# One layer of a hybrid decoder (sparse attention, gated delta rule, S5, MLP) on one core: another layout of the S5 input, another order of the parameter work, the state stores and the attention bursts

## The chip, the cores and the metric

The program runs on one core of one Trainium2 chip. The metric is the device time of one execution in microseconds; the median of three runs of the kernel before is 2086.05 (2082.03 to 2086.13). Engines are named as in the profile: PE (TensorE) multiplies matrices, PEld is its weight load, DVE is VectorE, ACT is ScalarE, POOL is GpSimd, SP is SyncE, which issues most DMAs.

## The reference

A prompt of 1024 tokens and eight samples of eight tokens (1088 tokens in all, width 1024) go through one layer with the same weights:

- `h = rmsnorm(x)`; one projection `h @ w_in` gives the columns of three mixers.
- Attention, 8 query heads on 2 key/value heads of 64: a compressed branch over means of blocks of 64 keys, a selected branch over the best 16 blocks, a window of 512; three softmaxes with ALiBi, added by gates. With 1024 prompt tokens there are 16 blocks, so the selected branch sees every block before the query.
- A gated delta rule (4 heads of 64) behind a short convolution over four tokens; the last three pre-convolution rows of each sequence are outputs (the convolution states).
- S5, 16 groups of 16 channels with 64 complex states each: `h_t = A h_{t-1} + B u_t`, `y_t = Re(C h_t) + D u_t`, then GELU and a gated linear unit. The last states are outputs.
- `x += concat(mixers) @ w_out`, `x += relu(rmsnorm(x) @ up)^2 @ down`, a last rmsnorm. Key/value rows, window buffers and states are outputs too.

Everything is float32; large products are split into three products of rounded parts (high x high, low x high, high x low).

## The kernel before

The program is a row of blocks, each with one instruction stream for each engine and a barrier behind it: input norm with the feature projection and S5 (`feature_and_s5`, to 251 us of the profile), query projection with the short convolution (from 280), token projection, delta rule, sample attention, prompt attention (`prompt_attention`, some 915 to 1184), then the output projection and the MLP (`project_and_mlp`). Nothing plans the order: each engine runs its stream in the order in which it is written, and semaphores hold it.

**Projections** (`project`, lines 437 to 510). A weight chunk of 128 columns is loaded by SP into one raw buffer, rounded by ScalarE into the high part (line 458) and subtracted by VectorE into the low part (line 475); the next chunk is loaded after that. A unit is one chunk times one of three column groups of the tokens (`GROUPS_N`), 24 matmuls (lines 393 to 395). With the first unit of a chunk ScalarE and VectorE make the next chunk. Units 0 to 5 are the two chunks of S5's input u, units 6 to 23 the six chunks of the delta rule's q, k and v. ScalarE evicts each unit from one of three PSUM banks (line 642).

**S5** is woven between the units by `S5.scalar`, `S5.vector`, `S5.tensor` and `S5.pool`. It works on blocks of eight tokens: 128 blocks of the prompt and 8 of the samples. VectorE makes the angles, the powers of A, and the input matrix from 13 loaded parameters (`angles`, `powers`, `input_matrix`), ahead of all units (`vector_first`, `scalar_first`). GpSimd makes C times the powers of A (lines 759 to 769) when the powers are there. VectorE makes B times the powers at unit 3 (`input_powers`, line 916), the phases of the blocks at unit 6, the scan over blocks at unit 9. TensorE multiplies after unit 10 (prompt) and 12 (samples) the input with B (`products`, line 1063), in four tiles of 32 rows, and after unit 16 the outputs (`outputs`): the input with a table of taps (line 1073, 128 x 128 weights) and the states with C times the powers (line 1078, four column tiles of 32). The input `uT` is laid down token by token; both lines read token t of every block, a step of eight elements.

**Stores** at the end of this block (`stores`): SP waits for the last eviction, issues one DMA for the prompt's and six for the samples' convolution states out of the work array, then the two S5 states, and waits until all have landed.

**Prompt attention** goes by units (tile of 128 queries, one of four head pairs), 32 in all. A round e, written out by `schedule`, has for each score piece (up to 512 keys) of unit e: TensorE's scores of the two key/value heads (line 1822), VectorE's bias and row maximum (line 1907), ScalarE's exponentials; and for unit e - 2: groups of two key steps, each turned by four transposes (line 1847), copied to SBUF by ScalarE or, every third, VectorE, and multiplied with the values one group later (line 1833). The last group of a unit is multiplied at once and the compressed branch is added (line 1856). Two PSUM banks take the transposes, two the output, four the scores. Between scores and transposes VectorE makes the factors of unit e - 1 in round e behind the rows of the first piece (line 1918), and then scales one of the four stretches of probabilities, GpSimd three (line 1991).

## Time and profile before

| what | us |
| --- | --- |
| median of the runs | 2086.05 |
| the profiled execution | 2087.14 |
| its span, first to last instruction | 2085.3 |
| PE busy | 1838.9 (88%) |
| PEld busy | 1618.2 (78%) |
| DVE busy | 927.3 (44%) |
| ACT busy | 545.1 (26%) |
| POOL busy | 394.7 (19%) |

The times of rows are those of the profiled execution, counted from the first instruction of its span; what lies around the span is 1.84 us. The share of an engine is a mean over the whole span. A matmul's duration in a row holds its passage through the array; how fast they follow one another is read from their starts. A float32 matmul is two instructions.

### The profile page before, as it was taken

What the parts mean: (1) busy time and instruction counts of PE and PEld (TensorE: products, weight loads), DVE (VectorE), ACT (ScalarE), POOL (GpSimd) and SP (SyncE); (2) the same over time, 40 slices, a digit from 0 to 9 for tenths busy, and PEclk for the clock granted to TensorE, in tenths of its full rate; (3) what the DMA queues carried; (4) which work ended last, traced back from release to release, by engine and by line L of the source; (5) the groups of instructions that cost most, each with busy time, mean ns of one, the idle gap of its engine ahead of it and who ended that gap; (6) DMA issues with size and microseconds to landing.
All of it is one profiled execution on the core that took longest, in us unless ns stands there. A gap on an engine that the chain in (4) does not pass through costs nothing. (4 is left out here: it accounts for less than half of the span.)

```text
span 2085.3 us, 29782 instructions
## 1 busy us (share of the span) xinstructions
PE 1838.9 (88%) x12570; PEld 1618.2 (78%) x12570; DVE 927.3 (44%) x1767; ACT 545.1 (26%) x1069; POOL 394.7 (19%) x337
## 2 busy tenths in 40 slices
PE   6599868945999976668999799999999999999998
PEld 5598768945888866455555599988888899999986
DVE  6850054102444442235666435345544444444447
ACT  5111122112222212226565503321111111111122
POOL 2300000003344320016666300200000011111110
PEclk8789979976999986559999999999999999999999
DMA  3000241032000002010000210111111111111112
GB/s 126 30 22 11 12 54 42 22 112 81 1 1 1 26 2 69 10 71 1 1 2 1 78 51 23 56 54 41 41 41 41 42 60 41 41 41 41 41 41 86
DMA packets 35327, 81.30 MB, mean 39 GB/s; under 512 B 13658, under 2 KB 21946, under 8 KB 29914
## 3 DMA queue, kind: packets, MB, share of 16 engines
q1 hardware_dynamic: 32690, 73.53, 11.8%
q10 hardware_dynamic: 1976, 4.92, 0.6%
q8 instruction: 99, 1.62, 0.3%
q0 software_dynamic: 528, 0.95, 0.2%
q14 instruction: 34, 0.28, 0.0%
HBM read 71.36 MB, written 10.12 MB: 39 GB/s over the span
## 5 line engine op out<-in xcount | busy, mean ns | idle before, releaser
L393 PE MATMUL ps<-mlp_mix_hi,mlp_w_hi 128*128 128x364 f32 (+1 forms) x768 | 252.2, 328 | 0.0
L394 PE MATMUL ps<-mixT_lo,mlp_w_hi 128*128 128x364 f32 (+1 forms) x768 | 252.0, 328 | 0.0
L395 PE MATMUL ps<-mlp_mix_hi,w_lo 128*128 128x364 f32 (+1 forms) x768 | 251.7, 328 | 0.0
L2428 DVE TENSOR_TENSOR x<-x,ps 128x512 f32<-128x512 f32 (+1 forms) x288 | 181.4, 656 | 140.8 <-PE ps L395 139.3
L2408 POOL TENSOR_TENSOR mlp_rect<-mlp_rect 128x364 f32<-128x364 f32 (+1 forms) x96 | 77.7, 809 | 779.6 <-ACT mlp_rect L2350 779.6
L395 PE MATMUL ps<-mlp_w_hi,mlp_hid_lo 128*128 128x512 f32 x512 | 203.1, 397 | 0.0
L394 PE MATMUL ps<-w_lo,mlp_hid_hi_lo 128*128 128x512 f32 x512 | 202.9, 396 | 0.0
L393 PE MATMUL ps<-mlp_w_hi,mlp_hid_hi_lo 128*128 128x512 f32 x512 | 202.9, 396 | 0.0
L1991 POOL TENSOR_SCALAR pa_probs<-pa_probs,pa_fac 128x640 f32<-128x640 f32 (+7 forms) x96 | 159.2, 1671 | 222.2 <-DVE pa_fac L1918 222.2
L2350 ACT ACTIVATE mlp_rect<-ps 128x364 f32<-128x364 f32 (+1 forms) x96 | 45.7, 476 | 557.2 <-PE ps L395 554.3
L2468 DVE TENSOR_TENSOR mlp_hid_lo<-mlp_rect,mlp_hid_hi_lo 128x364 fp32r<-128x364 f32 x64 | 53.2, 831 | 234.4 <-ACT mlp_hid_hi_lo L2356 234.4
L393 PEld LDWEIGHTS ps<-mlp_mix_hi,mlp_w_hi 128*128 128x128 f32 x768 | 144.9, 189 | 0.7
L394 PEld LDWEIGHTS ps<-mixT_lo,mlp_w_hi 128*128 128x128 f32 x768 | 144.4, 188 | 0.6
L395 PEld LDWEIGHTS ps<-mlp_mix_hi,w_lo 128*128 128x128 f32 x768 | 144.2, 188 | 0.0
L393 PEld LDWEIGHTS ps<-mlp_w_hi,mlp_hid_hi_lo 128*128 128x128 f32 x512 | 96.5, 188 | 23.6
L394 PEld LDWEIGHTS ps<-w_lo,mlp_hid_hi_lo 128*128 128x128 f32 x512 | 96.5, 188 | 23.6
L395 PEld LDWEIGHTS ps<-mlp_w_hi,mlp_hid_lo 128*128 128x128 f32 x512 | 96.4, 188 | 23.5
L1833 PE MATMUL ps<-pa_PT,tokens 128*64 128x128 f32 x1056 | 89.2, 290 | 16.9 <-DVE pa_PT L1930 13.0
L2003 ACT ACTIVATE pa_probs<-pa_probs,pa_nm 128x640 f32<-128x640 f32 (+7 forms) x128 | 92.8, 728 | 31.6 <-DVE pa_nm L1907 31.6
L1847 PEld LDWEIGHTS ps<-ident,pa_probs 128*128 128x128 f32 x528 | 57.1, 144 | 56.5 <-issue 52.3
L1258 POOL TENSOR_TENSOR dn_B<-dn_AT,dn_level 128x512 f32<-128x512 f32 (+1 forms) x59 | 73.6, 1264 | 127.9 <-DVE dn_aqkT L1393 47.9
L2418 DVE TENSOR_TENSOR w_lo<-w_raw,mlp_w_hi 128x2048 fp32r<-128x2048 f32 x36 | 82.4, 2288 | 24.9 <-ACT mlp_w_hi L2325 24.9
(465 smaller groups left out, 3862.5 us busy)
## 6 DMA issues: line engine op xcount, KB each, us to landing
w_raw<-in_w_up SPq DMA_DIRECT2D x16, 1024.0 KB, 4.7
w_raw<-in_w_down SPq DMA_DIRECT2D x16, 1024.0 KB, 4.7
feat_raw<-in_w_feat SPq DMA_DIRECT2D x12, 512.0 KB, 3.6
uT<-in_w_token SPq DMA_DIRECT2D x4, 1056.0 KB, 5.3
ck<-in_cache_nsa SPq DMA_DIRECT2D x16, 256.0 KB, 3.0
w_raw<-in_w_out SPq DMA_DIRECT2D x4, 1024.0 KB, 6.5
x<-in_x_prompt SPq DMA_DIRECT2D x4, 1024.0 KB, 8.3
out_y_p<-x SPq DMA_DIRECT2D x8, 512.0 KB, 2.6
```

The lines of the kernel that those rows point to most:

```text
L393: pe.matmul(out, lhs[0], rhs[0], start=first, stop=False)
L394: pe.matmul(out, lhs[0], rhs[1], start=False, stop=False)
L395: return pe.matmul(out, lhs[1], rhs[0], start=False, stop=last)
L1258: pool.tensor_tensor(B[:n, x, :, :n], AT[:n, k % 4, :, :n], mask, ALU.mult).then_inc(b_ready, 1)
L1833: last = pe.matmul(m.ps[64 * g:64 * g + 64, 6 + i % 2, r * P:(r + 1) * P], values[:, g * HD:(g + 1) * HD], PT[:, st % PTN, (2 * s + g) * P ...
L1847: last = pe.transpose(m.ps[:, 4 + st % 2, (2 * s + g) * P:(2 * s + g + 1) * P], probs[:, slot(e, g), col:col + P], m.ident[:])
L1991: last = pool.tensor_scalar(probs[:, x, o:o + w], probs[:, x, o:o + w], fac[:, x, b:b + 1], None, ALU.mult)
L2003: act.activation(probs[:, x, o:o + w], probs[:, x, o:o + w], ACT.Exp, bias=nm[:, x, b, pieces(i)[j][1]:pieces(i)[j][1] + 1], scale=-1.0, a ...
L2408: pool.tensor_tensor(part, part, part, ALU.mult).then_inc(rect_squared, 1)
L2418: dve.tensor_tensor(w_lo[:, s, :], w_raw[:, s, :], w_hi[:, s, :], ALU.subtract).then_inc(w_lo_made, 1)
L2428: dve.tensor_tensor(part, part, bank, ALU.add).then_inc(done, 1)
L2468: dve.tensor_tensor(hid_lo[:, g % 2, f, o:o + w], part, hi, ALU.subtract).then_inc(hidden_lo, 1)
```

## The change

- `GROUPS_N` becomes 368, 360 and 360 columns wide, multiples of eight.
- S5's input is laid down with the token's place in its block as the outer index: the six evictions of units 0 to 5 read PSUM with a step of eight, and the products and outputs read contiguous blocks.
- The S5 parameters move from ahead of unit 0 to behind the eviction of unit 0 on ScalarE, and behind the rounding of the second weight chunk on VectorE.
- GpSimd's C powers move to VectorE (`output_powers`, at unit 6, behind the fourth chunk); the phases move from unit 6 to unit 7.
- The S5 states are stored before the last load of SP in the block. GpSimd copies the convolution states into two small arrays, feature chunk by feature chunk behind the evictions, and two DMAs store them. The block waits for the S5 states alone; SP of the query block waits for the other two at its end.
- In prompt attention a round has batches: up to two score pieces, up to three groups of transposes, then the values of the batch before. Three PSUM banks take the transposes and one the output; six slots instead of four hold the turned probabilities. The factors follow the rows of the first batch. ScalarE evicts a tile's output in the first batch of the next unit.

```diff
-GROUPS_N = [(0, 364), (364, 364), (728, 360)]
+GROUPS_N = [(0, 368), (368, 360), (728, 360)]
...
             sp.dma_start(m.token_raw[0], m.w_in[FEAT]).then_inc(m.token_raw[1], 16)
+            sp.wait_ge(m.sem("proj_stored"), 16 * 2)
...
             if c < 2:
-                dst = m.uT[:, c, o:o + w]
+                dst = s5.uT[:, c, :, o // 8:(o + w) // 8]
+                src = src.rearrange("p (b t) -> p t b", t=8)
...
+            s5.store(sp)
             sp.wait_ge(evac[0], len(units) - 2)
             sp.dma_start(m.query_raw[0][:], m.w_in[0]).then_inc(m.query_raw[1], 16)
-            sp.wait_ge(evac[0], len(units))
-            sp.wait_ge(conv_put, 7)
-            sp.dma_start(m.conv_prompt, m.dnx[:, :, SEQ:SEQ + 3]).then_inc(stored, 16)
-            for f in range(6):
-                sp.dma_start(m.conv_sample[:, f],
-                             m.dnx[:, f, 3 + SEQ:].rearrange("p (b s) -> p b s", b=NB)[:, :, NQ:NQ + 3]
-                             ).then_inc(stored, 16)
-            s5.store(sp)
-            sp.wait_ge(stored, 16 * 7)
+            sp.wait_ge(conv_kept, 12)
+            sp.dma_start(m.conv_prompt, m.conv_last[:]).then_inc(conv_stored, 16)
+            sp.dma_start(m.conv_sample, m.convbuf[:]).then_inc(conv_stored, 16)
+            sp.wait_ge(s5.stored, 32)
...
             s5.pool(pool)
+            pool.wait_ge(conv_put, 7)
+            for f in range(6):
+                pool.wait_ge(evac[0], 3 * (f + 2) + 3)
+                pool.tensor_copy(m.conv_last[:, f], m.dnx[:, f, SEQ:SEQ + 3]).then_inc(conv_kept, 1)
+                pool.tensor_copy(m.convbuf[:, f], m.dnx[:, f, 3 + SEQ:].rearrange("p (b s) -> p b s", b=NB)[:, :, NQ:NQ + 3]
+                                 ).then_inc(conv_kept, 1)
...
     def scalar(self, act, u):
         m = self.m
+        if u == 0:
+            self.scalar_params(act)
...
     def vector(self, dve, u):
+        if u == 0:
+            self.link = Link(dve, self.vec)
+            self.angles(dve)
+            self.powers(dve)
+            self.input_matrix(dve)
         if u == 3:
             self.input_powers(dve)
         if u == 6:
+            self.output_powers(dve)
+        if u == 7:
             self.phases(dve)
...
+    def output_powers(self, dve):
+
+        T, ca, cw, t, tt, link = self.T, self.ca, self.cw, self.hold_t, dve.tensor_tensor, self.link
+        c = lambda ri: self.over_k(cw[:, ri], T)
+        dve.wait_ge(self.neg_made, 1)
+        for ri, op in ((0, ALU.add), (1, ALU.subtract)):
+            tt(ca[:, ri], c(ri), self.power(0, 1, T + 1), ALU.mult)
+            link(tt(t, c(1 - ri), self.power(1, 1, T + 1), ALU.mult))
+            last = tt(ca[:, ri], ca[:, ri], t, op)
...
-                                         self.m.uT[rows, ct, tokens.start + t:tokens.stop:self.T], start=t == 0, stop=t == self.T - 1,
+                                         self.uT[rows, ct, t, blocks], start=t == 0, stop=t == self.T - 1,
...
-                pe.matmul(bank[:, e * n:(e + 1) * n], self.tb[:, ct, t, :], self.m.uT[:, ct, p - t::self.T],
+                pe.matmul(bank[:, e * n:(e + 1) * n], self.tb[:, ct, t, :], self.uT[:, ct, p - t, :],
...
-        PTN = 4
+        PTN, TURNS = 6, 3
...
-            if e >= len(UNITS):
-                return [(None, range(n))]
-            k = len(pieces(UNITS[e][0]))
-            return [(j, range(n * j // k, n * (j + 1) // k)) for j in range(k)]
+            k = len(pieces(UNITS[e][0])) if e < len(UNITS) else 0
+            parts = max((k + 1) // 2, (n + TURNS - 1) // TURNS)
+            return [(range(min(k, 2 * j), min(k, 2 * j + 2)), range(n * j // parts, n * (j + 1) // parts)) for j in range(parts)]
...
-                    if k == 0 and r == 0 and i >= 2:
-                        pe.wait_ge(o_out, i - 1)
+                    if k == 0 and r == 0 and i:
+                        pe.wait_ge(o_out, i)
...
+                held = []
                 for e in ROUNDS:
...
-                    for j, ks in schedule(e):
-                        if j is not None:
+                    for js, ks in schedule(e):
+                        for j in js:
                             scores(e, j)
                         for k in ks:
                             turn(e - LAG, k)
+                        for k in held:
+                            multiply(*k)
+                        held = [(e - LAG, k) for k in ks]
...
-                    for j, ks in schedule(e):
-                        if j is not None:
+                    for n, (js, ks) in enumerate(schedule(e)):
+                        for j in js:
                             rows(e, j)
-                        if (j or 0) == 0 and 1 <= e <= len(UNITS):
+                        if n == 0 and 1 <= e <= len(UNITS):
                             factors(e - 1)
                             scale(e - 1)
...
+                        if e - LAG - 1 >= 0 and UNITS[e - LAG - 1][1] == R - 1 and ks and ks[0] == 0:
+                            outputs(UNITS[e - LAG - 1][0])
```

## Rows read from the trace of the kernel before

**Rows 1.** Waits of PE, 0 to 300 us: total us, times, longest.
```profile
PE ps L393 <- DVE qp_wlo L475: 29.8, 1, 29.8
PE ps L393 <- DVE fp_wlo L475: 26.6, 1, 26.6
```

**Rows 2.** Timeline of DVE, S5 parameters: start, us, instruction.
```profile
49.18 3.51 DVE L890 TENSOR_TENSOR s_v<-s_par 128x8 f32<-128x8 f32 x1
...
56.32 0.17 DVE L892 TENSOR_TENSOR s_v<-s_v 128x8 f32<-128x8 f32 x1
```

**Rows 3.** Timeline of POOL at the same time, of ACT at unit 4.
```profile
49.03 3.64 POOL L764 TENSOR_TENSOR mixT_raw<-s_cw,s_ak 128x2048 f32<-128x2048 f32 x1 [19.51 <-DVE s_ak L876]
...
87.76 0.48 ACT L642 ACTIVATE uT<-ps 128x364 f32<-128x364 f32 x1 [3.52 <-PE ps L395]
```

**Rows 4.** Timelines at the block barriers near 278 and 331 us.
```profile
267.51 0.43 SPq L745 DMA_DIRECT2D out_s_s<-s_fin_s  x1
277.98 1.06 ACT L458 ACTIVATE qp_whi<-feat_raw 128x1024 fp32r<-128x1024 f32 x1 [26.89 <-PEq L437]
...
329.84 1.07 DVE L562 TENSOR_SCALAR qT<-ps 64x360 f32<-64x360 f32 x2 [2.23 <-PE ps L395]
331.20 0.33 POOL L538 MEMSET tokens<- 64x288 f32 x1 [52.18 <-POOLq L437]
```

**Rows 5.** Windows: length, PE, PEld, DVE, ACT, POOL busy (instructions), PEclk, DMA, GB/s.
```profile
77.30:82.00 4.70, 4.67 (x15) 4.67 (x16) 0.00 (x0) 1.05 (x1) 0.00 (x0) 0.50 0.33 112
83.10:107.80 24.70, 24.70 (x161) 24.65 (x160) 24.01 (x52) 7.73 (x17) 0.00 (x0) 1.00 0.14 44
143.50:151.50 8.00, 8.00 (x156) 8.00 (x152) 7.62 (x10) 0.00 (x0) 0.00 (x0) 0.50 0.01 4
940.00:1184.00 244.00, 229.08 (x1972) 137.90 (x1970) 141.02 (x480) 138.13 (x301) 148.30 (x81) 0.99 0.01 1
```

**Rows 6.** Groups of DVE, B times the powers: busy us, mean ns, idle before.
```profile
L916 DVE TENSOR_TENSOR s_bat<-s_bb,s_ak 128x1792 f32<-128x1792 f32 x2 | 4.0, 2021 | 0.0
```

**Rows 7.** Timeline of PE in the S5 outputs.
```profile
174.76 7.64 PE L1073 MATMUL ps<-uT,s_bat 128*128 128x136 f32 x30
182.33 1.60 PE L1078 MATMUL ps<-s_hp,mixT_raw 128*32 128x136 f32 x48
183.86 7.65 PE L1073 MATMUL ps<-uT,s_bat 128*128 128x136 f32 x30
```

**Rows 8.** Groups, 0 to 330 us: S5 products of the prompt.
```profile
L1063 PE MATMUL ps<-uT,s_bat 32*128 32x128 f32 x256 | 15.2, 408 | 0.0
```

**Rows 9.** Timeline of PE in attention, tile 5, and its last unit.
```profile
1088.16 0.66 PE L1847 MATMUL ps<-ident,pa_probs 128*128 128x128 f32 x4
1088.74 0.66 PE L1833 MATMUL ps<-pa_PT,tokens 128*64 128x128 f32 x8
1089.33 1.13 PE L1822 MATMUL ps<-kwinT,qT 64*128 64x512 f32 x4
1090.39 0.66 PE L1847 MATMUL ps<-ident,pa_probs 128*128 128x128 f32 x4
...
1175.60 1.09 PE L1847 MATMUL ps<-ident,pa_probs 128*128 128x128 f32 x8
```

**Rows 10.** Waits of PE, 905 to 1185 us.
```profile
PE ps L1833 <- DVE pa_PT L1930: 13.0, 25, 1.9
```

**Rows 11.** Groups of attention: score rows on DVE, scaling on POOL.
```profile
L1907 DVE CUSTOM_DVE_ANT_0 pa_probs<-ps,pa_dwin 128x512 f32<-128x512 f32 x40 | 26.0, 688 | 10.7 <-PE ps L1822 10.7
...
L1991 POOL TENSOR_SCALAR pa_probs<-pa_probs,pa_fac 128x640 f32<-128x640 f32 x36 | 68.8, 1921 | 13.6 <-DVE pa_fac L1918 13.6
```

**Rows 12.** Timeline of DVE: factors of units 8, 24 and 31.
```profile
953.61 0.16 DVE L1918 TENSOR_TENSOR pa_fac<-pa_rs,tokens 128x4 f32<-128x4 f32 x1
...
1087.40 0.16 DVE L1918 TENSOR_TENSOR pa_fac<-pa_rs,tokens 128x4 f32<-128x4 f32 x1
...
1165.42 0.16 DVE L1918 TENSOR_TENSOR pa_fac<-pa_rs,tokens 128x4 f32<-128x4 f32 x1
```

More of the change, by code:

```diff
@@ L607, in feature_and_s5 @@
     with ExitStack() as ctx:
[L608 to L609 removed]
+        conv_in, conv_put, conv_kept = m.sem("conv_in"), m.sem("conv_put"), m.sem("conv_kept")
+        conv_stored = m.sem("proj_stored")
         units = [(c, n) for c in range(8) for n in range(3)]
@@ L719, in __init__ @@
         sem = lambda n: m.sem(f"s5_{n}")
-        self.loaded, self.vec, self.vec_pool, self.e1, self.e2 = (sem(n) for n in ("loaded", "vec", "vec_pool", "e1", "e2"))
+        self.loaded, self.vec, self.e1, self.e2 = (sem(n) for n in ("loaded", "vec", "e1", "e2"))
         self.trig_in, self.trig, self.neg_made = sem("trig_in"), sem("trig"), sem("neg_made")
@@ L921, in input_powers @@
         last.then_inc(self.ba_made, 1)
+    def output_powers(self, dve):
[6 more added lines that the diff above has]
+            last = tt(ca[:, ri], ca[:, ri], t, op)
+            if ri == 0:
+                link(last)
+        last.then_inc(self.ca_made, 1)
     def phases(self, dve):
@@ L1019, in tensor @@
             pe.wait_ge(self.u_out[0], 6)
-            self.products(pe, slice(0, SEQ), self.NBLK).then_inc(self.g_prod, 1)
+            self.products(pe, slice(0, self.NBLK), self.NBLK).then_inc(self.g_prod, 1)
         if u == 11:
@@ L1033, in tensor @@
             pe.wait_ge(self.g_read, 1)
-            self.products(pe, slice(SEQ, TOK), NB).then_inc(self.gs_prod, 1)
+            self.products(pe, slice(self.NBLK, self.COLS), NB).then_inc(self.gs_prod, 1)
         if u == 16:
@@ L1053, in tensor, with products @@
                 last.then_inc(self.glu, 1)
-    def products(self, pe, tokens, n):
+    def products(self, pe, blocks, n):
         for ri in range(2):
@@ L1832, in multiply @@
                         for g in range(G):
-                            last = pe.matmul(m.ps[64 * g:64 * g + 64, 6 + i % 2, r * P:(r + 1) * P], values[:, g * HD:(g + 1) * HD],
+                            last = pe.matmul(m.ps[64 * g:64 * g + 64, 7, r * P:(r + 1) * P], values[:, g * HD:(g + 1) * HD],
                                              PT[:, st % PTN, (2 * s + g) * P:(2 * s + g + 1) * P], start=k + s == 0, stop=False,
@@ L1836, in multiply @@
                     last.then_inc(pv_step, 1)
+                    if k == len(groups(e)) - 1:
+                        for g in range(G):
+                            last = pe.matmul(m.ps[64 * g:64 * g + 64, 7, r * P:(r + 1) * P], vcp[:, 4 * g + r, :],
+                                             cmp_T[:, i, :], start=False, stop=True, skip_group_check=True)
+                        last.then_inc(pv_done, 1)
                 def turn(e, k):
@@ L1842, in turn @@
                         pe.wait_ge(scaled_pool, e + 1)
-                    if st >= 2:
-                        wait_for_copy(pe, st - 2)
+                    if st >= TURNS:
+                        wait_for_copy(pe, st - TURNS)
                     for s, (col, _) in enumerate(groups(e)[k]):
                         for g in range(G):
-                            last = pe.transpose(m.ps[:, 4 + st % 2, (2 * s + g) * P:(2 * s + g + 1) * P],
+                            last = pe.transpose(m.ps[:, 4 + st % TURNS, (2 * s + g) * P:(2 * s + g + 1) * P],
                                                 probs[:, slot(e, g), col:col + P], m.ident[:])
                     last.then_inc(turned, 1)
-                    if k:
-                        multiply(e, k - 1)
-                    if k == len(groups(e)) - 1:
-                        multiply(e, k)
-                        i, r = UNITS[e]
-                        for g in range(G):
-                            last = pe.matmul(m.ps[64 * g:64 * g + 64, 6 + i % 2, r * P:(r + 1) * P], vcp[:, 4 * g + r, :],
-                                             cmp_T[:, i, :], start=False, stop=True, skip_group_check=True)
-                        last.then_inc(pv_done, 1)
                 def cmp_scores():
@@ L1889, in _ @@
                             turn(e - LAG, k)
+                        for k in held:
+                            multiply(*k)
+                        held = [(e - LAG, k) for k in ks]
                     if e == 0:
                         cmp_scores()
+                for k in held:
+                    multiply(*k)
             @block.vector
@@ L2023, in _ @@
                                 copy(st)
+                        if e - LAG - 1 >= 0 and UNITS[e - LAG - 1][1] == R - 1 and ks and ks[0] == 0:
+                            outputs(UNITS[e - LAG - 1][0])
                         for b in range(2):
-                            if j is not None and j == last_piece(UNITS[e][0], b):
+                            if js and last_piece(UNITS[e][0], b) in js:
                                 exps(e, b)
@@ L2034, in _ @@
                                            ACT.Copy).then_inc(cmp_out, 1)
-                    if e >= LAG and UNITS[e - LAG][1] == R - 1:
-                        outputs(UNITS[e - LAG][0])
+                outputs(TS - 1)
 def sample_attention(nc, m):
```

44 lines of the change are left out of this document (13 added, 31 removed).

## The prediction

> **What bounds the kernel now.** I read the waits of TensorE first. In the first 300 us it waits long only twice: 26.6 us for the rounded weights of the second chunk of the first block, and 29.8 us for the first weights of the query projection [rows 1]. Then the timelines of the engines that end these waits. VectorE, which must make the weights' low part, was making S5 parameters instead: eight-element operations that take 0.17 us alone took 3.5 us each, and beside each stood a 3.64 us operation of GpSimd, the powers of C [rows 2, 3]. The second wait ends with a block's barrier: ScalarE sat 26.89 us on it while SP issued small stores of states [rows 4]. The stage table of windows says the rest: in the S5 part TensorE issues without a pause, in attention (940 to 1184) it is busy 229 of 244 us at a clock of 0.99, and no other engine is over 149 [rows 5]. So in the first part everything that TensorE loses or does is on the path, and in attention one must ask what TensorE's busy time is made of. The MLP after 1184 is untouched.
>
> **The sum** is made against the profiled execution, 2087.14 us (span 2085.3 and 1.8 around it); the median of the runs is 2086.05, 1.1 lower.
>
> **Weights ahead of parameters, no GpSimd powers.** The second chunk's rounding now stands before the parameters on ScalarE and VectorE, so the wait of 26.6 us goes. It also left TensorE at its lower level (0.50) until 82.0 [rows 5]: half of 4.7 us, 2.4, goes too. What is late next? VectorE runs the parameters some 2 us later; without GpSimd beside it they end near 56 instead of 76 (six operations at 0.17 instead of 3.5 to 4.3). The third chunk's low part follows at once; TensorE wants it at 63 (51 plus three units of 4.0, an eviction's 0.48 and the 3.52 before it [rows 3]). The six power operations move to VectorE: 2048 elements at the rate of 1792 in 2.02 us [rows 6] are 2.3 each, 13.9 in all (above, 3.6 to 4.5 each as on GpSimd, 24). They stand after the fourth chunk's low part and before the 11.5 us of phases. VectorE's work from 83.1 to 107.8 had no gaps [rows 5], so I lay it end to end: input powers 57 to 70, C powers to 85, phases to 96, the fifth low part at 97. TensorE, laid likewise (51, units of 4.0, transposes, products), asks for it at about 104. Cover 7 us; at the upper price 3 us would be lost. I take 0 and gain 29.0.
>
> **Token in its block as outer index.** The moving operand of the S5 products and outputs was read with a step of eight elements and is now contiguous. Outputs: 30 instructions of 136 columns start at 174.76 and end at 182.33, 252 ns each; the neighbouring line, 136 contiguous columns in four column tiles at once, has 48 in 1.53 us, 127 ns for each four, change of kind included [rows 7]. 144 such instructions at 125 ns less are 18.0 us. Products: 256 of 128 columns in 15.2 us are 237 ns for four row tiles at once [rows 8]; at 127, 64 fours lose 7.0. Bounds: nothing (the weight load decides) and 19 plus 8. The nearest row has the same columns and differs in the step and in the tiles' width; I take it: 25.0. The sample products (8 columns) stay. The price is on ScalarE: six evictions read PSUM in steps. No row shows that; between nothing and twice their 0.48, three us in all, beside TensorE units of 4.0 each: 0.
>
> **Gathered stores.** Seven DMAs after the last eviction become two (576 and 72 bytes for each partition, contiguous), the S5 stores go ahead of the query weights' load, and the block no longer waits for the convolution states: the query block's SP does, behind its last load, where nothing is queued. The load of query weights waits for eviction 22 as before; the S5 states were ready some 80 us earlier, so the wait ahead of it costs nothing. New at the end: GpSimd's two copies after the last eviction (0.4) and two issues, 0.65 and 0.45, on SP. At another barrier the next block's first instruction starts 0.3 us after the last one [rows 4]. So ScalarE starts at 251.1 + 0.1 + 0.4 + 0.1 + 1.1 + 0.3 = 253.1 on the old scale, not at 277.98: 24.8. (Bounds: 26.5 if the copies hide, 14 if the barrier still stood 10.5 us behind its last store, as 277.98 does behind 267.51 [rows 4].)
>
> **Group widths** 368, 360, 360 instead of 364, 364, 360: the same columns, 0.
>
> **Attention.** A burst is a run of score, transpose or value matmuls. Four transposes to the next burst take 0.58, eight value matmuls 0.59, a 512-column score piece 1.06; but eight transposes in a row are busy 1.09 where four are 0.66 [rows 9]. So four more cost 0.43, and each change of kind 0.16. Eight have a wait between them (line 1844), so it is the change that costs, not the wait. From the code, the old order has 328 bursts and the new 157. TensorE also waits 13.0 us for copies before value matmuls [rows 10]; held back a batch, these find their copies. An upper end: 171 x 0.16 + 13 = 40.
> But the rounds are coupled. A unit's factors need the next round's score rows, then GpSimd scales three blocks, and then the transposes start, two rounds later. For tile 6 the work of a round is 1536 columns of scores at 0.90 for 512, 2.70; twelve steps of transposes and as many of values, 5.16; the compressed term 0.21. With 15 changes and one 0.4 copy wait that is 10.9 before; tile 7 in the same way 11.8 with 17. Measured from the factors at 1087.40 to those at 1165.42, four rounds of tile 6 and three of tile 7: 78.0, 11.15 each [rows 12]; the formula gives 11.3. After: 6 and 8 changes, 9.0 and 10.0.
> The loop of two rounds after: the rest of the round behind the first transposes (9.0 less two score pieces and a change, 1.74), the first piece 1.06, VectorE's rows of two pieces (0.69 for 512 columns [rows 11], 2.5 for four), factors and hand-overs 0.8, GpSimd 896 + 640 + 640 elements in proportion to 640 in 1.92 [rows 11], 6.7: 18.4, or 9.2 a round. Tile 7 gives 9.9, under its 10.0. So (4 x 9.2 + 3 x 10.0) is 66.8 against 78.0: 11. For tiles 2 to 5 the loop decides and gives 5.5, 6.95, 8.05 and 8.8 a round (work 4.6, 6.25, 7.7, 8.4); four of each are 117, where 953.61 to 1087.40 took 133.8 [rows 12]: 17. The last unit: factors at 1165.42 to the end at 1184 are 18.6; after, GpSimd 7.1 and a round of 7.6 give 15: 3. Tiles 0 and 1: nothing. Together 31; I take 30, bounds 0 (the second piece's rows delay the factors by what the changes save) and 43 (all changes, all waits, a denser start). The single output bank is free after one 0.6 us ScalarE copy, behind which TensorE has a batch of scores and transposes.
>
> **Sum:** 29.0 + 25.0 + 24.8 + 30 = 108.8. 2087.1 less 108.8 is 1978.3; on the median's scale 1977.
>
> **Rivals.**
> 1. Attention keeps its pace, since the loop through factors and GpSimd decides everywhere. For it: in tiles 2 and 3 the loop is within half a us of the old round. Against: for tiles 6 and 7 adding up TensorE's own pieces reproduces the rounds. 1977 + 30 = 2007.
> 2. Contiguous reads give nothing, the weight load of 128 columns decides. For it: the contiguous neighbour loads 32 columns only. Against: attention's transposes load 128 columns and cost 0.43 for four [rows 9]. 1977 + 25 = 2002.
> 3. The moved VectorE work is late for TensorE in the S5 part (C powers at GpSimd's price, a wait at the fifth chunk): up to 10 us, 1980 to 1987.
> 4. Slower than before: the granted clock falls in attention. Work on few columns can do this: in 143.5 to 151.5 TensorE is busy 8.00 of 8.00 us with 8-column products and stands at 0.50, 1.2 GHz [rows 5]. So can idleness, which left it at 0.50 until 82.0, and bursts followed by a wait for GpSimd make the idle spells longer in tiles 1 to 3. Streaming in attention is 33,792 score columns at 0.90 for 512, 132 groups of two steps twice at 0.43, and 32 compressed terms at 0.21: 180 us. At half clock it takes 180 more, less some 25 of waits that it fills: 1977 + 155 = 2132; from 0.7 of the streaming on, the kernel is slower than before. In a mild form only tiles 1 to 3 run so: 50 us of streaming, less 12 rounds with 1 us of wait each, 1977 + 38 = 2015. Against both: 940 to 1184 holds 0.99 with waits in it.
> The Trainium skill (TensorE: Matmul & The Clock Gate, Part 1) says that TensorE drops to its lower clock after an idle spell and regains it under sustained work, which speaks for the mild form. The trace agrees on idleness, by the 0.50 until 82.0, and adds that busy work on few columns lowers it too.
>
> **Chances.** Forecast 0.62 (own range 1962 to 1992), rival 1 0.14, rival 2 0.06, rival 3 0.09, rival 4 in full 0.02, its mild form 0.04, something overlooked that makes it slower 0.01. The range must reach rivals 1 and 2 and, below, 43 instead of 30 in attention with the upper ends of the reads: 1955 to 2009. Measurement tells about 0.2%, 4 us, from no change. Between rival 4's forms lies no change, 0.02. So slower 0.03, the same 0.02, faster 0.95.
>
> **What would show it.** No wait of TensorE over 2 us between 51 and the block's end; VectorE's parameters at 0.17 each; the outputs' line at about 115 to 127 ns an instruction, the products' fours the same; ScalarE's barrier wait near 2.5 us; attention's changes of kind halved, rounds of 9 to 10 us for tiles 6 and 7, and TensorE's transposes waiting for GpSimd in tiles 2 to 5. Wrong would be: a wait for the low weights at the third or fifth chunk, 237 ns products, rounds over 10.8 in tile 6, or a clock under 0.9 in attention.

## The result, and the profile after

The changed kernel takes 1964.8 us (median of 4 runs, 1957.95 to 1967.41), the kernel before 2084.4 (4 runs): a ratio of 0.942, interval 0.939 to 0.945. It is faster by 120 us. The forecast was 1977, range 1955 to 2009. The profiled execution took 1963.47 us, span 1961.6; its span is 123.7 shorter than that of before, against 108.8 in the forecast's sum:

| stretch (from and to TensorE's instructions) | before | after | gained | forecast |
|---|---|---|---|---|
| start to the last product of the first block | 250.5 | 193.2 | 57.3 | 29.0 + 25.0 |
| from there to the first query product | 29.8 | 4.8 | 25.0 | 24.8 |
| to the first transposes of attention | 639.0 | 638.9 | 0.0 | 0 |
| attention, first transposes to the last compressed term | 264.7 | 226.3 | 38.4 | 30 |
| MLP, first to last product | 887.0 | 884.3 | 2.6 | 0 |
| the ends | 14.3 | 14.0 | 0.3 | 0 |

The waits of TensorE, 0 to 300 us, answer [rows 1]:

```profile
PE ps L393 <- DVE kvp_wlo L475: 5.8, 1, 5.8
...
PE ps L393 <- DVE qp_wlo L475: 4.8, 1, 4.8
```

The 26.6 us for `fp_wlo` are gone, and of 29.8 for the first query weights 4.8 are left (`kvp_wlo` belongs to the block behind the query projection). The timelines, in order of time, answer [rows 2, 4 and 7]:

```profile
49.70 0.17 DVE L885 TENSOR_TENSOR s_v<-s_par 128x8 f32<-128x8 f32 x1
...
55.01 1.22 DVE L475 TENSOR_TENSOR fp_wlo<-feat_raw,fp_whi 128x1024 fp32r<-128x1024 f32 x1
...
134.53 3.74 PE L1081 MATMUL ps<-uT,s_bat 128*128 128x136 f32 x30
138.20 0.68 PE L1086 MATMUL ps<-s_hp,mixT_raw 128*32 128x136 f32 x16
...
194.56 0.43 SPq L653 DMA_DIRECT2D out_conv_s<-convbuf  x1
...
195.66 1.06 ACT L458 ACTIVATE qp_whi<-feat_raw 128x1024 fp32r<-128x1024 f32 x1 [1.90 <-PEq L437]
```

The parameter that took 3.51 us takes 0.17; the third chunk's low part begins at 55.0 (forecast 56). The thirty output products that took 7.57 us to the next line take 3.67 (134.53 to 138.20), 122 ns each instead of 252. ScalarE sits 1.90 us on the barrier, not 26.89. The groups of S5 products, to set beside [rows 8]; columns as there:

```profile
L1081 PE MATMUL ps<-uT,s_bat 128*128 128x136 f32 x144 | 18.2, 283 | 0.0
L1071 PE MATMUL ps<-uT,s_bat 32*128 32x8 f32 x256 | 11.6, 319 | 0.0
L1071 PE MATMUL ps<-uT,s_bat 32*128 32x128 f32 x256 | 7.4, 272 | 0.0
```

The prompt's products went from 15.2 to 7.4 us: 116 ns for four. The mean of 283 ns is not the time from one instruction to the next: the next starts while one is still on its way. 18.2 us for 144 are 126 ns from start to start, changes of kind included.

Windows over all of attention, before and after (the columns of [rows 5]; PEclk is the granted clock of TensorE as a share of 2.4 GHz, so 0.50 is 1.2), and the wait that is left to the transposes after:

```profile
919.30:1184.00 264.70, 245.93 (x2074) 149.40 (x2072) 150.74 (x535) 148.90 (x338) 157.35 (x93) 0.96 0.01 1
```

```profile
836.90:1063.30 226.40, 207.85 (x2074) 153.21 (x2072) 150.49 (x537) 142.62 (x339) 156.85 (x93) 0.98 0.01 1
```

```profile
PE ps L1860 <- issue: 15.5, 17, 2.0
```

The same 2074 matmuls keep TensorE busy 38.1 us less; it is idle 18.5 us, as it was (18.8). So the gain is all busy time: the 13.0 us of waits for copies [rows 10] are gone, but 15.5 us before transposes have taken their place. Counted from the first transposes, the bursts (runs of matmuls of one kind) fell from 327 to 156. The factors of units 8, 24 and 31, to set beside [rows 12], and two bursts of a round of tile 6 with what starts the transposes of tile 3:

```profile
865.89 0.17 DVE L1928 TENSOR_TENSOR pa_fac<-pa_rs,tokens 128x4 f32<-128x4 f32 x1
...
888.16 4.93 POOL L2001 TENSOR_SCALAR pa_probs<-pa_probs,pa_fac 128x512 f32<-128x512 f32 x3 [2.15 <-DVE pa_fac L1928]
893.19 0.30 PE L1860 MATMUL ps<-ident,pa_probs 128*128 128x128 f32 x1 [1.98 <-issue]
...
983.69 0.16 DVE L1928 TENSOR_TENSOR pa_fac<-pa_rs,tokens 128x4 f32<-128x4 f32 x1
...
1004.00 1.53 PE L1860 MATMUL ps<-ident,pa_probs 128*128 128x128 f32 x12
1005.46 1.53 PE L1840 MATMUL ps<-pa_PT,tokens 128*64 128x128 f32 x24
...
1046.32 0.51 DVE L1928 TENSOR_TENSOR pa_fac<-pa_rs,tokens 128x4 f32<-128x4 f32 x1
```

From the factors of unit 8 to those of unit 24 it takes 117.8 us (forecast 117), from there to those of unit 31 62.6 (forecast 66.8). GpSimd ends at 893.09 and the transposes start at 893.19. The trace puts their idle time before it down to "issue" and names no engine, but in the program the instruction waits for VectorE's scaling and for GpSimd's, and GpSimd's ends last. For 23 of the 31 units behind the first, the transposes start within 0.16 us of its end.

### The profile page after: what moved, and what is told of

The parts are those of the page before. It is cut to its first block and busy times, and to the rows that moved or that the text cites. A ratio compares the mean times of both kernels' runs of the same rounds, so it can differ in the third digit from the quotient of the medians.

```text
span 1961.6 us, 29787 instructions
## 1 busy us (share of the span) xinstructions
PE 1768.7 (90%) x12570; PEld 1600.6 (82%) x12570; DVE 918.1 (47%) x1773; ACT 537.9 (27%) x1069; POOL 374.3 (19%) x343
## 3 DMA queue, kind: packets, MB, share of 16 engines
q1 hardware_dynamic: 25954, 73.53, 11.2%
## 5 line engine op out<-in xcount | busy, mean ns | idle before, releaser
L393 PE MATMUL ps<-mlp_mix_hi,mlp_w_hi 128*128 128x360 f32 (+1 forms) x768 | 252.5, 329 | 0.0
L395 PE MATMUL ps<-mlp_mix_hi,w_lo 128*128 128x360 f32 (+1 forms) x768 | 252.3, 328 | 0.0
L394 PE MATMUL ps<-mixT_lo,mlp_w_hi 128*128 128x360 f32 (+1 forms) x768 | 251.5, 327 | 0.0
L2419 POOL TENSOR_TENSOR mlp_rect<-mlp_rect 128x360 f32<-128x360 f32 (+1 forms) x96 | 77.5, 807 | 774.8 <-ACT mlp_rect L2361 774.8
L2361 ACT ACTIVATE mlp_rect<-ps 128x360 f32<-128x360 f32 (+1 forms) x96 | 45.5, 474 | 556.1 <-PE ps L395 553.2
L2479 DVE TENSOR_TENSOR mlp_hid_lo<-mlp_rect,mlp_hid_hi_lo 128x368 fp32r<-128x368 f32 (+1 forms) x64 | 53.1, 830 | 234.8 <-ACT mlp_hid_hi_lo L2367 234.8
L1860 PEld LDWEIGHTS ps<-ident,pa_probs 128*128 128x128 f32 x528 | 57.5, 142 | 37.4 <-issue 33.1
L393 PE MATMUL ps<-kvp_whi,h_hi 128*128 128x264 f32 x288 | 82.7, 287 | 5.8 <-DVE kvp_wlo L475 5.8
```

Of the source, the lines that this page charges most:

```text
L393: pe.matmul(out, lhs[0], rhs[0], start=first, stop=False)
L394: pe.matmul(out, lhs[0], rhs[1], start=False, stop=False)
L395: return pe.matmul(out, lhs[1], rhs[0], start=False, stop=last)
L1860: last = pe.transpose(m.ps[:, 4 + st % TURNS, (2 * s + g) * P:(2 * s + g + 1) * P], probs[:, slot(e, g), col:col + P], m.ident[:])
L2361: act.activation(rect[:, (rank[u] - 1) % 2, :w], m.ps[:, bank_of(u), :w], ACT.Relu).then_inc(rectified, 1)
L2419: pool.tensor_tensor(part, part, part, ALU.mult).then_inc(rect_squared, 1)
```

## The experiments

Theory: the gain is four separate sums, each with the mechanism of the forecast. All kernels are the changed kernel with one edit. The kernel before had medians from 2079.0 to 2084.4 beside the result and the four groups of runs, so runs are compared by their ratio to it, and "more" or "less" than the changed kernel is (ratio - 0.9422) x 2084. The last column is read from the profiled execution of each run, the first block from its first product. The intervals of params_first, block_waits, single_pieces, pool_relief2 and by_tile touch or overlap that of the changed kernel (0.939 to 0.945): their medians alone do not tell them from it, and what is said of them rests on the trace.

| run | ratio, interval | against the changed kernel | in the trace, at its place |
|---|---|---|---|
| old_layout | 0.956, 0.953 to 0.958 | +28 us | +26.5 products and outputs |
| steps | 0.950, 0.948 to 0.952 | +16 | +13.3 first block |
| pool_powers | 0.954, 0.952 to 0.957 | +25 | +19.6 first block (elsewhere +3.3 attention) |
| params_first | 0.947, 0.945 to 0.949 | +10 | +8.7 first block |
| seven_stores | 0.951, 0.949 to 0.954 | +19 | +11.2 barrier, +5.2 query block (elsewhere +2.4 first block, +3.4 attention) |
| block_waits | 0.944, 0.940 to 0.947 | +3, not told from 0 | +1.1 barrier |
| old_attention | 0.960, 0.958 to 0.962 | +37 | +37.3 attention |
| single_pieces | 0.946, 0.944 to 0.949 | +9 | +10.6 attention |
| not_held | 0.964, 0.962 to 0.966 | +45 | +44.5 attention |
| pool_relief | 0.934, 0.932 to 0.935 | -18 | -12.0 attention |
| pool_relief2 | 0.939, 0.936 to 0.941 | -7 | -8.0 attention |
| by_tile | 0.937, 0.935 to 0.939 | -11 | -13.1 attention |

**The reading step.** First the old layout alone, then a step of two elements for column block 0 and of four for block 1.

```
-                dst = s5.uT[:, c, :, o // 8:(o + w) // 8]
-                src = src.rearrange("p (b t) -> p t b", t=8)
+                dst = m.uT[:, c, o:o + w]
...
-        self.uT = m.uT[:].rearrange("p c (t b) -> p c t b", t=self.T)
+        self.uT = m.uT[:].rearrange("p c (b t) -> p c t b", t=self.T)
```

> The changed kernel with the S5 input laid down by tokens again, so that the moving operand is read with a step of eight elements. Theory (the step alone makes the reads slow, and nothing hides it): the 144 output products go back from about 122 to 252 ns, the 64 fours of prompt products from 115 to 237 ns, so 18.7 + 7.8 = 26.5 us more than the changed kernel: 1991 us. Rival A (the new layout also costs something elsewhere, in ScalarE's evictions with a step): less than 26.5 comes back, 1985 to 1989. Rival B (the pace came from another edit): the durations stay and the time is 1965.

```profile
144.10 7.64 PE L1080 MATMUL ps<-uT,s_bat 128*128 128x136 f32 x30
151.67 1.60 PE L1085 MATMUL ps<-s_hp,mixT_raw 128*32 128x136 f32 x48
```

The outputs are back at 252 ns (7.57 for 30), the prompt's products at 15.2 us. The two lose 18.7 and 7.8, 26.5 as expected. Rival A falls too: ScalarE's six evictions with a step took 454 to 481 ns in the changed kernel, the contiguous ones of before 447 to 478, and TensorE waited for neither.

```
-        self.uT = m.uT[:].rearrange("p c (t b) -> p c t b", t=self.T)
+        self.uT = [m.uT[:, c, :].rearrange("p (h b l) -> p h l b", h=self.T // s, l=s) for c, s in enumerate((2, 4))]
...
```

`s` is the step, in elements, with which TensorE reads column block 0 (two) and 1 (four).

> The changed kernel with the S5 input of column block 0 laid so that TensorE reads it with a step of two elements (8 bytes), and of block 1 with a step of four (16 bytes). Theory 1 (two elements in a 16-byte line suffice): block 0 keeps 122 ns an output and 115 a four of products, block 1 goes to 252 and 237; 72 x 0.130 + 32 x 0.122 = 13.3 us more: 1978 us. Theory 2 (any step is slow): both at 252 and 237, 26.5 us more: 1991 us. Theory 3 (the cost goes with the share of a line that is used): block 0 in between, near 165 and 155, 17 to 18 us more: 1982.5 us.

```profile
139.63 3.89 PE L1082 MATMUL ps<-uT,s_bat 128*128 128x136 f32 x30
...
154.49 7.53 PE L1082 MATMUL ps<-uT,s_bat 128*128 128x136 f32 x30
```

The first line is of block 0, the second of block 1. Step two: 3.82 us for 30, 127 ns; step four: 7.46, 249 ns (from a line's start to the next line's). Products and outputs together take 13.2 us more, where theory 1 has 13.3. The Trainium skill (Advanced Engine Details and Errata, SBUF Cachelines) says that SBUF has 16-byte lines and that at least two hits on a line are needed for full speed. Two float32 of a line are two hits, and the trace agrees: 127 ns against 122 with all four, and 249 with one.

**GpSimd's powers and the order of the weights.**

```
     def pool(self, pool):
+        self.output_powers(pool)
...
         if u == 6:
-            self.output_powers(dve)
-        if u == 7:
             self.phases(dve)
```

With the powers gone from VectorE, the phases stand at unit 6 again.

> The changed kernel with the six power operations back on GpSimd, the weights still rounded ahead of the parameters. Theory (VectorE's small parameters are slow because GpSimd works beside them, wherever they stand): seven of them take 3.5 to 4.3 us again, the parameters end 22 us later, near 76.5 instead of 55.0, and the wait moves from the second chunk to the third: TensorE asks for the third low part at about 60 and gets it at 77.7, 17 us of wait and 2 to 3 us at the lower clock: 1985 us. Rival (the order of weights and parameters was the whole cause): no wait over 2 us for the third chunk, 1965 us.

```profile
48.93 3.65 POOL L924 TENSOR_TENSOR mixT_raw<-s_cw,s_ak 128x2048 f32<-128x2048 f32 x1 [20.02 <-DVE s_ak L870]
...
49.08 3.52 DVE L884 TENSOR_TENSOR s_v<-s_par 128x8 f32<-128x8 f32 x1
...
76.04 1.22 DVE L475 TENSOR_TENSOR fp_wlo<-feat_raw,fp_whi 128x1024 fp32r<-128x1024 f32 x1
```

TensorE waited 17.5 us once, for the third chunk (expected 17): the parameters' price goes with GpSimd, the order only decides which chunk is late. The total is 5 above the expectation; 3.3 of it lie in attention, which this edit does not touch, with two 3.4 us spells at clock 0.5 in tile 3. The changed kernel itself shows the same price at another place, where nothing waited for it: a copy of 16 elements, 0.17 us before, takes 3.45 beside a long operation of GpSimd.

```profile
113.53 4.66 POOL L764 TENSOR_TENSOR s_bat<-s_bw,s_quarter 128x2048 f32<-128x2048 f32 x1 [84.35 <-PE ps L1071]
...
114.77 3.45 DVE L980 COPY s_fin_p<-s_hp 128x16 f32<-128x16 f32 x1
```

```
+                 ... "scalar_first": s5.scalar_params, "vector_first": s5.vector_params, ...
...
     def vector(self, dve, u):
-        if u == 0:
-            self.link = Link(dve, self.vec)
...
```

The parameters stand ahead of the unit loop again (`scalar_first`, `vector_first`), the powers stay on VectorE.

> The changed kernel with the parameters ahead of the second chunk's rounding again, the powers still on VectorE. Theory (GpSimd beside VectorE was most of the stall, the order the smaller part): parameters of 11 us end at 54.5, the low part at 55.8, TensorE asks at about 48 to 51 and waits 5 to 7 us; 1970 to 1973 us. Rival (the order was the whole cause): the wait of 26.6 us is back, 1992 us.

```profile
PE ps L393 <- DVE fp_wlo L475: 5.0, 1, 5.0
```

```profile
55.23:62.06 6.83, 6.22 (x20) 6.22 (x21) 2.15 (x3) 1.06 (x1) 0.00 (x0) 0.50 0.25 77
```

The wait is as expected, and the first block is 8.7 us longer. From 55.23, just before the wait ended, to 62.06 the clock stood at 0.50; TensorE was busy 6.22 us of it, so at half speed the wait of 5.0 us cost some 3 us more. The 3.4 us spell at 0.50 from 41.58 came before the wait and stands in other runs too (before, seven_stores), so it is not the wait's.

**The stores.** Gathering and deferring, one at a time.

```
-            sp.wait_ge(conv_kept, 12)
-            sp.dma_start(m.conv_prompt, m.conv_last[:]).then_inc(conv_stored, 16)
-            sp.dma_start(m.conv_sample, m.convbuf[:]).then_inc(conv_stored, 16)
...
+            sp.dma_start(m.conv_prompt, m.dnx[:, :, SEQ:SEQ + 3]).then_inc(conv_stored, 16)
+            for f in range(6):
+                sp.dma_start(m.conv_sample[:, f],
...
```

GpSimd's copies are out too; the S5 states are still stored early, and the query block still does the waiting for the convolution states.

> The changed kernel with the seven small convolution stores straight from the features again, not gathered by GpSimd; their landing is still waited for in the query block. Theory (the issue of many small packets holds SP and with it the barrier): in the trace of before the seven issues took from 251.12 to 263.3 us, 12.2 us, the last two 5.07 and 3.81 each; the gathered two and their copies take 1.4; so the query block starts 10.8 us later: 1976 us. Rival (waiting for the landing was the whole cost, issues are cheap): seven issues at 0.6 us, 3 us more: 1968 us.

```profile
197.72 11.89 SPq L655 DMA_DIRECT2D out_conv_s<-dnx  x6
...
210.08 1.06 ACT L458 ACTIVATE qp_whi<-feat_raw 128x1024 fp32r<-128x1024 f32 x1 [13.07 <-PEq L437]
```

The waits of this run, and ScalarE's wait for the same load in the changed kernel:

```profile
PE ps L393 <- DVE qp_wlo L475: 21.0, 4, 16.0
ACT qp_whi L458 <- DMA feat_raw<-in_w_feat: 13.3, 1, 13.3
```

```profile
ACT qp_whi L458 <- DMA feat_raw<-in_w_feat: 4.8, 1, 4.8
```

Theory, and more than its price: the issues hold the barrier 11.2 us longer, and then ScalarE waits 13.3 us for the load of the second query chunk where it waited 4.8, and the query block takes 5.2 us more. The load is issued as soon behind the barrier as in the changed kernel (2.3 us after ScalarE's first instruction), but a 12 KB load of GpSimd's at that time took 11.9 us to land instead of 2.1: a deferred wait does not take the stores' packets out of the way. The other 5.8 us of this run lie where the edit is not: 3.4 in attention, with two spells at 0.5 in tile 3 as in pool_powers, and 2.4 in the first block, with a 3.4 us spell at 0.5 at 42 us.

The query block's first product comes 16.0 us after the first block's last one here, 29.8 before the change and 4.8 with it. So of the 25.0 us gathering is worth 11.2; the other 13.8 came from storing the S5 states early and from not waiting for the landing, and no run separates these two.

```
 sp.wait_ge(s5.stored, 32)
+sp.wait_ge(conv_stored, 32)                     # block_waits
```

> The changed kernel, the two gathered stores as they are, but the first block waits for their landing again. Theory (gathered stores land fast, so the deferred wait was the smaller part): two stores of 9 and 72 KB land 2 to 3.5 us after their issue, 2 to 3.5 us more: 1967 to 1968.5 us. Rival (a store's landing takes some 10 us, as the S5 states took 10.1 in the trace of before): 10 us more, 1975 us.

```profile
196.72 1.06 ACT L458 ACTIVATE qp_whi<-feat_raw 128x1024 fp32r<-128x1024 f32 x1 [2.97 <-PEq L437]
```

ScalarE sits 2.97 us on the barrier instead of 1.90: once the stores are gathered, deferring their wait is worth 1.1 us, less than the 2 to 3.5 expected.

**Attention.** Old schedule in the changed kernel (the functions of before, line by line):

```
-PTN, TURNS = 6, 3
+PTN = 4      ... and schedule, turn, multiply, outputs of before
```

> The changed kernel with the old attention schedule. Theory (attention's gain is its own and adds to the others): the span from the first transposes to the end goes from 226.3 back to 264.7, 38.4 us more: 2003 us; tiles 0 and 1 take 38.6 from the first transposes to those of unit 8 instead of 33.2. Rival (part of the 38.4 comes from the granted clock's start in attention, which depends on what ran ahead): between 30 and 36 comes back, 1995 to 2001.

Attention takes 263.6 us instead of 226.3: 37.3 of the 38.4 come back, so attention's gain adds to the others. The first eight units took 37.5 (38.6 before, 33.2 in the changed kernel); the rest of the 38.4 lies there.

```
-            parts = max((k + 1) // 2, (n + TURNS - 1) // TURNS)
-            return [(range(min(k, 2 * j), min(k, 2 * j + 2)), ...
+            parts = max(k, (n + TURNS - 1) // TURNS)
+            return [(range(min(k, j), min(k, j + 1)), ...
```

> The changed attention with bursts of one score piece instead of two; values are still held back a batch. A round of tiles 4 to 7 then has 12 changes of kind and two for the compressed term instead of 6 to 8. Theory 1 (a change costs TensorE 0.16 us and TensorE's bursts set the rounds of tiles 4 to 7): rounds 0.6 to 1.0 us longer in tiles 4 to 7, 12 us more: 1977 us; transposes of tile 6 no longer start 0.1 us behind GpSimd. Theory 2 (GpSimd's loop sets the rounds everywhere): VectorE makes the factors after one piece's rows instead of two, about 1.25 us earlier in a loop of two rounds, so 0.6 us less a round and 10 us less: 1955 us.

```profile
835.60:1072.50 236.90, 227.34 (x2074) 147.51 (x2072) 152.62 (x537) 146.66 (x338) 157.18 (x93) 0.99 0.01 1
```

277 bursts instead of 156, and TensorE is busy 227.34 instead of 207.85 us: 19.5 / 121 is 0.161 us a change, the 0.16 of the forecast. The rounds of tiles 4 to 7 are 0.63 to 0.80 us longer (tile 6: 10.1 instead of 9.3). Theory 2 falls. Only 10.6 of the 19.5 reach the end, since TensorE is idle less, 9.6 us instead of 18.5: part of the time that the changes take was a wait for GpSimd before. The three kinds also differ in the shape of their tiles (64*128, 128*128 and 128*64). The Trainium skill (TensorEngine Tiling (Array Packing), Key Properties) says that changing the tiling mode drains TensorE. The trace agrees in that a change costs time, 0.161 us here; how much of it is due to the tile shape no run shows.

```
-                        for k in held:
-                            multiply(*k)
-                        held = [(e - LAG, k) for k in ks]
+                        for k in ks:
+                            multiply(e - LAG, k)
...
```

> The changed attention, but the value matmuls of a batch follow right behind its own transposes instead of a batch later. The changes between kinds of matmul stay as few. Theory 1 (holding back is a large part of the gain, since a batch's first value matmul would wait for a copy that starts only with the batch): 52 batches wait 0.2 to 0.6 us each, 20 us more in attention (10 to 30): 1985 us. Theory 2 (the fewer changes of kind are the gain; the 13.0 us of copy waits of before lay beside GpSimd's loop): 0 to 5 us more, 1965 to 1970 us.

```profile
PE ps L1840 <- DVE pa_PT L1936: 31.0, 27, 2.5
PE ps L1840 <- ACT mixT_raw L2021: 6.3, 7, 1.2
...
PE ps L1860 <- issue: 2.7, 5, 1.2
```

```profile
837.20:1108.00 270.80, 225.34 (x2074) 158.43 (x2072) 148.77 (x535) 143.24 (x338) 157.15 (x93) 0.95 0.01 1
```

Theory 1, and twice its price: with as few bursts as the changed kernel (157) attention is longer than before. VectorE makes every third copy, and in its order the copies stand behind the batch's score rows and the scaling; the value matmuls wait 31.0 us for them. In [rows 10] it was 13.0. They also wait 6.3 us, seven times, for ScalarE to empty the single output bank, which the changed kernel does behind a batch of other work. Of the 44.5 us, 27.0 are idle time of TensorE (45.5 us instead of 18.5, though it hardly waits before transposes any more: 2.7 us, 15.5 in the changed kernel) and 17.5 busy time. The clock has a part in the latter: it stands at 0.5 for 29 us of this stretch, 24 of them in six spells after it first rose, and for 8 us in the changed kernel; at half speed that is at most some 10 us. The rest of the busy time stays open.

**Towards a faster kernel.** If GpSimd's loop sets the rounds of the changed kernel, work taken off GpSimd must shorten them.

```
+                    for b, (o, w) in enumerate(branches(UNITS[e][0])):
...
-                    for g, b in ((1, 0), (1, 1), (0, 1)):
+                    for g, b in ((1, 0), (1, 1)):
```

The first loop is VectorE's, which now scales both stretches of the first head, the second is GpSimd's.

> The changed kernel with the third of GpSimd's three scalings of a unit (the window of the first head, up to 640 columns, 1.92 us) done by VectorE. Theory (the loop factors, GpSimd, transposes sets the rounds of tiles 2 to 6, half of its length a round): tile 2 goes from 5.4 to 4.8 a round, tile 3 from 7.0 to 6.25, tile 4 from 8.07 to 7.7, tile 5 from 8.76 to 8.4, tile 6 from 9.2 to 9.0, where TensorE's own work takes over, and the last unit's tail is 1.9 shorter: 9 + 2 = 11 us less, 1954 us. Rival A (TensorE's own bursts set the rounds already): 0 to 2 us. Rival B (VectorE's longer scaling delays the score rows and copies): as long as before or up to 8 us longer, 1965 to 1973 us.

```profile
829.50:1043.80 214.30, 208.79 (x2074) 153.13 (x2072) 174.51 (x566) 143.94 (x338) 111.05 (x62) 0.98 0.01 2
```

Attention is 12.0 us shorter (expected 11): tiles 2 to 6 take 2.75, 2.48, 1.08, 1.04 and 0.62 less, with TensorE idle 5.5 us instead of 18.5. The moved scaling of 640 columns, 1.88 us on GpSimd, takes 1.30 to 1.41 on VectorE, twice what was expected, but VectorE had the time. The ratio of 0.934 is below that of the changed kernel with its interval apart. Of the 18 us between the runs 12 are the edit's; most of the rest lies in a stretch that the edit does not touch (last section).

```
+                    for g, b in ((0, 0), (0, 1), (1, 1)):
...
+                    for g, b in ((1, 0),):
```

> GpSimd scales one of a unit's four stretches only, VectorE the other three (in the changed kernel three and one, in the run with one stretch moved two and two). Theory (after one stretch was moved TensorE sets the rounds of tiles 4 to 7, the loop through GpSimd those of tiles 0 to 3): the loop is 1.92 - 0.65 = 1.3 us shorter, 0.4 us a round in tiles 0 to 3 and 1.3 us at the tail, tiles 4 to 7 as they are: 7 to 8 us less than with one stretch moved, attention about 207 us, 1938 us. Rival (VectorE, at 131 of 164 us, becomes the bound: 12 us more of work there delay its copies and score rows): attention 214 to 222 us, 1945 to 1952 us.

```profile
834.80:1053.10 218.30, 209.89 (x2074) 152.12 (x2072) 187.50 (x599) 144.12 (x338) 68.10 (x31) 0.99 0.01 2
```

The rival: VectorE, busy 187.5 of 218.3 us, becomes late. TensorE waits 4.7 us for its copies and 3.2 for its scaling, 0.7 and 0 with one stretch moved. Tiles 0 and 1 gain 2.2 us against that run, tiles 2 to 7 lose 6.1, so attention is 3.9 us longer.

```
+                    for g, b in ((0, 0), (0, 1)) + (((1, 1),) if UNITS[e][0] < 2 else ()):
...
+                    for g, b in ((1, 0),) if i < 2 else ((1, 0), (1, 1)):
```

> The best split by tiles: VectorE scales three of a unit's four stretches in tiles 0 and 1, where the run with three was shorter (12.12 and 15.44 us instead of 13.85 and 15.93), and two from tile 2 on, where the run with two was shorter. Theory (the tiles' rounds are independent of each other): 1.7 + 0.5 us less than with two everywhere, attention about 212 us, median 1942 us, no difference from 1944 that can be measured. Rival (tile 2 starts later for it, or the gain of tile 0 was the granted clock's start): attention 213 to 215 us.

Attention takes 213.2 us, 1.1 less than with two everywhere, at the edge of the rival's 213 to 215: tile 0 keeps its gain of 1.7, but tile 1 took 16.5, not 15.4, so the tiles are not independent; that the hand-over to tile 2 does it was not shown. In the medians no gain is seen: four of its five runs took 1950 to 1953 us and one 1942, and pool_relief had 1944.4.

## Why the prediction was right

**Weights and powers.** The step held: the wait gone, parameters at 0.17, the low part at 55.0, no chunk late, C powers on VectorE at 2.28 to 2.29 (forecast 2.3). Over the seven units from 41 us on 30.3 us went, forecast 29.0; undone one at a time, the move of the powers costs about 20 and the order about 9. The difference of 1.3 fits a 3.4 us spell at 0.50 at 41 us in the profile of before, which the changed kernel's did not have: the unit in it took 5.65 us instead of 4.10. One reading was kinder than the result: the fifth chunk was to have 7 us of cover (ready at 97, asked for at 104). VectorE was ready earlier, at 95.56, but TensorE, whose products had become faster, asked at 98.00, so 2.4 us were left. At the forecast's upper price for the powers, 10 us more, some 8 us would have been lost by this estimate, and not 3.

```profile
94.33 1.23 DVE L475 TENSOR_TENSOR fp_wlo<-feat_raw,fp_whi 128x1024 fp32r<-128x1024 f32 x1
...
98.00 0.33 PE L395 MATMUL ps<-h_hi,fp_wlo 128*128 128x368 f32 x1
```

**Layout.** 18.7 + 7.8 measured, 18.0 + 7.0 forecast: the neighbouring row in four column tiles was a fair price (127 ns; it is 122 and 116). Rival 2, that the weight load decides, is false: with the same weights loaded, the step alone moves the outputs between 122 and 252 ns.

**Stores.** 25.0 for 24.8. The parts: gathering is worth about 16 (11.2 at the barrier, 5.2 by the late load), and once it is done the deferred wait 1.1. The sum went straight to where ScalarE would start and did not need the parts, but its idea that a deferred wait frees what follows is only half true: with seven stores the next load pays.

**Group widths.** 0, as said. The MLP's 2.6 us are not theirs: the products of 512 columns, whose shape did not change, carry them; why they do stays open.

```profile
L393 PE MATMUL ps<-mlp_w_hi,mlp_hid_hi_lo 128*128 128x512 f32 x512 | 202.1, 395 | 0.0
```

Three such groups are 606.3 us after and 608.9 before (203.1, 202.9 and 202.9); the groups of 360 to 368 columns are 756.1 after and 755.9 before.

**Attention.** The step was right (changes of kind at 0.16, and values held back), the size too small: 38.4 against 31 worked out and 30 taken. Of the 38.1 us of busy time, 171 changes of kind at 0.161 are 27.5; the clock, at its lower level for 19 us of attention before and 8 after, is at most 6 more; the rest was not taken apart. From the factors of unit 8 to the end it gave 33.1 (forecast 31): 16.0, 15.4 and 1.7 where the forecast had 17, 11 and 3. Tile 6's rounds took 9.21 us (forecast 9.2). The round from the factors of unit 30 to those of unit 31 took 5.8 instead of 10.0, since no score rows stand ahead of the last factors; but GpSimd, still at unit 30, began unit 31 only 1.85 us after them, and the tail took 16.9 instead of 15. So the two errors partly cancel. The term that was mis-sized is "Tiles 0 and 1: nothing": 5.4 us. Tile 1 gave 1.3 with the clock at its full level in both; tile 0 gave 4.1, part of it by the clock, which rose 16.0 us after the first transposes before and 8.1 after them in the changed kernel. With the same schedule it rose 2.2 us after them in old_layout, and tile 0 took 13.2 there instead of 15.1: this part is a matter of the run, and luck as far as the size of the gain goes.

**Rivals.** Attention keeping its pace is false, but its mechanism is what remains: GpSimd's loop sets most rounds, and pool_relief shows 12 us of it. VectorE was not late. The clock did not fall for good; a small case of its mild form was seen in other runs of the same schedule (pool_powers, seven_stores: two spells, tile 3 longer by 3.1 and 3.2 us). What was not tested by itself: the place of the factors behind two pieces, the third transpose bank and the six slots.

## What to carry to other kernels

Price each change between kinds of matmul and each strided read from two neighbouring rows of the trace, then sum by stage; here these sums added, stage by stage. The moving operand need not be a contiguous row: in these float32 products a step of two elements cost nearly nothing (127 ns against 122), a step of four as much as one of eight (249 and 252). When a stall ends with an engine that does small slow things, look at who works beside it; and after each gain name the loop that is next (here GpSimd's scaling) and move work only until its new owner is the bound.

## What the runs showed of the hardware

- The stretch from the token block to attention, the same code in every run, takes from 469.6 us, where the granted clock stands at its lower level for 187 us of it (pool_relief), to 476.5 us, where it does for 207 (by_tile). The last 130 us of it in the changed kernel and in block_waits (columns as in [rows 5]):

```profile
700.00:832.60 132.60, 85.32 (x714) 72.87 (x714) 36.36 (x118) 31.15 (x101) 2.97 (x4) 0.54 0.18 59
```

```profile
700.85:826.80 125.95, 78.05 (x711) 67.10 (x710) 35.24 (x116) 30.67 (x101) 2.97 (x4) 0.58 0.19 62
```

This alone is 6.7 us between two runs, more than the 4 us that the forecast took as the least that can be told from no change.

- Six stores of 12 KB in small packets took SP 11.89 us to issue (seven_stores; the first four 0.59 to 0.64 each, the last two 5.92 and 3.35) where two gathered ones took 0.33 and 0.43: the cost stands at the issuing engine and, by the load that was late behind them, in the queue.
- Behind a wait of 5.0 us TensorE worked 6.2 us at clock 0.50 (params_first), behind one of 26.6 us 4.7 [rows 5].
- VectorE operations of 8 and 16 elements that take 0.17 us alone took 3.45 to 4.35 us where a GpSimd operation of 2048 elements was running, and ended with it: at 52.60 us where GpSimd's ended at 52.58 (pool_powers), at 118.22 where it ended at 118.19 (the changed kernel).
